# Scan levels of a chunked recurrence: a narrower wait on TensorE, K made in halves by ScalarE, two levels of block copies moved to ScalarE

## What is computed

```python
f = lb + (1.0 - lb) * jax.nn.sigmoid(f_raw);  k = 1.0 - f;  v = i_in
# S_t = diag(f_t) S_{t-1} + k_t v_t^T,   o_t = S_t^T q_t
def step(S, inp):
    qb, kb, vb, gb = inp
    G = jnp.cumsum(gb, axis=-2)
    o_inter = jnp.einsum('bhtd,bhdv->bhtv', qb * jnp.exp(G), S)
    diff = G[:, :, :, None, :] - G[:, :, None, :, :]
    decay = jnp.exp(jnp.where(causal, diff, -jnp.inf))
    A = jnp.sum(qb[:, :, :, None, :] * kb[:, :, None, :, :] * decay, axis=-1)
    o = o_inter + jnp.einsum('bhts,bhsv->bhtv', A, vb)
    ...
```

## Time and profile before

| | |
|---|---|
| median of 3 runs | 2320.0 us (2317.55 to 2323.71) |
| the profiled execution's own time | 2319.5 us |
| its span | 2317.7 us |
| mean granted TensorE clock | 0.976 of full |
| busy: PE / DVE / ACT / POOL | 96% / 37% / 32% / 40% |
| chain that ended last: PE / issue / POOL / DVE / ACT | 60% / 23% / 11% / 4% / 1% |
| the ten levels, first product to the last q update's end | 1709.50 to 1801.76 us |

### The profile page before, as it was taken

How to read it: one execution, slowest core, us unless ns; L and a number is a source line. 1 busy time by engine, 2 the same in 40 slices (tenths; PEclk the granted TensorE clock), 3 DMA queues, 4 the chain that set the end, 5 groups by cost and what they waited for, 6 DMA issues and landing times.

```text
span 2317.7 us, 32862 instructions
## 1 busy us (share of the span) xinstructions
PE 2229.0 (96%) x12905; PEld 1931.1 (83%) x12905; DVE 864.1 (37%) x1286; ACT 750.5 (32%) x1098; POOL 932.4 (40%) x707
## 2 busy tenths in 40 slices
PE   6999999999999999999997999999988999999998
PEld 5888888777888778887876999999988699999887
DVE  4232202666555522222036222232159054555402
ACT  4333212435667433333133322112100323333213
POOL 3444444445220344445433334444335014454542
PEclk9999999999999999999998999999989879999999
DMA  4223222521000223232221222222210002322231
GB/s 154 91 90 97 92 101 91 157 69 59 1 1 2 82 73 96 93 100 91 90 91 55 91 91 90 91 91 90 73 37 1 19 19 84 99 90 90 91 100 64
DMA packets 150638, 178.99 MB, mean 77 GB/s; under 512 B 6949, under 2 KB 140430, under 8 KB 150558
## 3 DMA queue, kind: packets, MB, share of 16 engines
q1 hardware_dynamic: 150395, 177.83, 23.5%
q10 hardware_dynamic: 163, 0.04, 0.0%
HBM read 175.76 MB, written 2.10 MB: 77 GB/s over the span
## 4 chain that ended last, share of the span: by engine, by line
PE 60%; issue 23%; POOL 11%; DVE 4%; ACT 1%; SPq 1%; DMA 0%; POOLq 0%; DVEq 0%; ACTq 0%
PE ps L1628 38%; POOL wlo L621 11%; PE ps L1768 11%; PE ps L2132 2%; PE ps L2155 2%; PE ps L2038 2%; PE ps L2008 1%; PE ps L2024 1%; PE ps L1882 1%; DVE Ad L1542 0%; PE ps L2034 0%; PE ps L2006 0%; PE ps L2089 0%; DVE Tod L1568 0%; PE ps L1861 0%
## 5 line engine op out<-in xcount | busy, mean ns | idle before, releaser
L621 POOL TENSOR_TENSOR wlo<-raw,whi 128x512 fp32r<-128x512 f32 x638 | 838.4, 1347 | 1177.8 <-ACT whi L708 1177.7
L1628 PE MATMUL ps<-xh,whi 128*128 128x512 f32 (+2 forms) x2432 | 702.4, 335 | 23.0 <-DVE gateT L1419 10.2
L1628 PE MATMUL ps<-xh,wlo 128*128 128x512 f32 (+2 forms) x2432 | 699.9, 334 | 0.0
L1628 PE MATMUL ps<-xl,whi 128*128 128x512 f32 (+2 forms) x2432 | 696.9, 333 | 0.0
L708 ACT ACTIVATE whi<-raw 128x2048 fp32r<-128x2048 f32 x160 | 304.9, 1906 | 791.0 <-PE ps L1628 480.8
L1628 PEld LDWEIGHTS ps<-xh,whi 128*128 128x128 f32 x2432 | 414.9, 189 | 75.5 <-POOL wlo L621 8.7
L1628 PEld LDWEIGHTS ps<-xh,wlo 128*128 128x128 f32 x2432 | 413.5, 189 | 46.6 <-issue 1.9
L1628 PEld LDWEIGHTS ps<-xl,whi 128*128 128x128 f32 x2432 | 413.5, 189 | 45.8
L1768 PE MATMUL ps<-act_h,wlo 128*128 (+1 forms) x528 | 208.6, 395 | 0.0
L1768 PE MATMUL ps<-act_l,whi 128*128 (+1 forms) x528 | 208.6, 395 | 0.0
L1768 PE MATMUL ps<-act_h,whi 128*128 (+1 forms) x528 | 208.6, 395 | 0.0
(11 more groups left out here) (301 smaller groups left out, 2582.5 us busy)
## 6 DMA issues: line engine op xcount, KB each, us to landing
raw<-in_w_in SPq DMA_DIRECT2D x47, 1024.0 KB, 5.0
raw<-in_ffn_wg SPq DMA_DIRECT2D x22, 1024.0 KB, 5.2
raw<-in_ffn_wu SPq DMA_DIRECT2D x22, 1024.0 KB, 5.1
raw<-in_ffn_wd SPq DMA_DIRECT2D x22, 1024.0 KB, 4.9
raw<-in_w_up SPq DMA_DIRECT2D x22, 1024.0 KB, 5.1
raw<-in_w_down SPq DMA_DIRECT2D x11, 1024.0 KB, 4.9
raw<-in_w_out SPq DMA_DIRECT2D x8, 1024.0 KB, 5.4
raw<-in_ple_w_gate SPq DMA_DIRECT2D x4, 1024.0 KB, 5.3
```

The lines of the kernel that those rows point to most:

```text
L621: last = nc.gpsimd.tensor_tensor(wlo[:, slot, d], raw[:, slot, d], whi[:, slot, d].bitcast(F32), ALU.subtract)
L1628: last = mm(ps[:, j * banks + b, 0:n], w[:, k, e * P:(e + 1) * P], x[:, k, c0:c0 + n], start=(k == 0 and q == 0), stop=(k == KD - 1 and q ...
```

## The change

Three edits, and the counts of semaphores that follow from them.

1. At levels above 0, PE waits for `LEVEL_UP` of the level below less one: for the q update, not for the decay totals issued behind it. POOL's k update now waits for those totals itself (`lev_up`), which it had got through PE's wait.
2. K = 1 - Fg is made by ACT in two halves of four heads (`k_made`), behind ACT's rounding of a weight unit. PE waits for the half that holds the head (META for both). DVE's instruction is gone, and `lev_up` counts one less.
3. At levels 5 and 6 (runs of 32 and 64 tokens) ACT copies the products into `Ad`, with plain copies of whole blocks, two per head at level 5 and one at level 6. PE waits for their banks on `lev_cp`. DVE has no copy to make at these levels but still waits for the products before its q update.

```diff
--- before.py
+++ after.py
@@ -145,7 +145,7 @@
 
 def level_updates():
 
-    n, out = 1, {}
+    n, out = 0, {}
     for lv in range(-1, LEVELS):
         for g in range(2):
             n += 2 if 0 <= lv < LEVELS - 1 else 1
@@ -165,7 +165,8 @@
 X_BANK = [2, 3, 4, 5, 6, 7, 2, 3]
 LEVEL_SEQ = level_sequence()
 LEVEL_UP = level_updates()
-LEVEL_CP0 = sum(lv < 7 for lv, _, _ in LEVEL_SEQ)
+FIRST_CP = 5
+LEVEL_CP0 = sum(lv < FIRST_CP for lv, _, _ in LEVEL_SEQ)
 P2 = 5
 N_ROWS = sum(len(r) for r in ROWS[1:]) + 2 * len(HEAD_ROWS)
 N_CONST = 7
@@ -426,6 +427,7 @@
         lev_sel = sem("lev_sel")
         lev_up = sem("lev_up")
         lev_k = sem("lev_k")
+        k_made = sem("k_made")
         amx_mm = sem("amx_mm")
         amx_cp = sem("amx_cp")
         o2_mm = sem("o2_mm")
@@ -692,6 +694,8 @@
             for lv in range(LEVELS - 1):
                 for g in range(2):
 
+                    if lv:
+                        pool.wait_ge(lev_up, LEVEL_UP[lv - 1, g])
                     pool.wait_ge(lev_mm, 1 + max(i for i, (l, n, _) in enumerate(LEVEL_SEQ) if l == lv and n in range(HG * g, HG * (g + 1))))
                     k2, decay = k_update(lv, g)
                     nc.gpsimd.tensor_tensor(k2, k2, decay, ALU.mult).then_inc(lev_k, 1)
@@ -1041,7 +1045,19 @@
             for u in range(W_IN2 + 35, W_IN2 + 38):
                 hi_one(u)
 
+            act.wait_ge(tiles_done, used_count(W_IN2 + 35))
+            act.wait_ge(p2_free, P2 + 64)
+            for g in range(2):
+                heads = slice(HG * g, HG * (g + 1))
+                nc.scalar.activation(K[:, heads, :], Fg[:, heads, :], ACT.Copy, scale=-1.0, bias=1.0).then_inc(k_made, 1)
             for idx, (lv, n, bank) in enumerate(LEVEL_SEQ):
+                if FIRST_CP <= lv < 7:
+                    act.wait_ge(lev_mm, idx + 1)
+                    w = 1 << lv
+                    for r in range(0, P, 2 * w):
+                        last = nc.scalar.activation(Ad[r:r + w, n, :].rearrange("p (i t) -> p i t", i=TT)[:, :, r + w:r + 2 * w],
+                                                    ps[r:r + w, bank, :].rearrange("p (i t) -> p i t", i=TT)[:, :, r + w:r + 2 * w], ACT.Copy)
+                    last.then_inc(lev_cp, 1)
                 if lv >= 7:
                     act.wait_ge(lev_mm, idx + 1)
                     w = 256 if lv == 7 else 512
@@ -1521,7 +1537,6 @@
                 ins.then_inc(lev_up, 1)
                 dve.wait_ge(lev_up, up_n[0])
 
-            link(nc.vector.tensor_scalar(K[:], Fg[:], -1.0, 1.0, ALU.mult, ALU.add))
             nc.vector.memset(Am[:], 0.0).then_inc(az, 1)
             dve.wait_ge(az, 2)
             idx = 0
@@ -1536,7 +1551,7 @@
                     if lv < 7 and n == META:
                         nc.vector.copy_predicated(Am[:], levelmask[0:M, lv + 1, 0:M].unsqueeze(1).to_broadcast([M, VH, M]),
                                                   ps[0:M, bank, 0:VH * M].rearrange("p (n m) -> p n m", n=VH)).then_inc(lev_sel, 1)
-                    elif 0 <= lv < 7:
+                    elif 0 <= lv < FIRST_CP:
                         second = lambda x: x.rearrange("p (i b e w) -> p i b e w", i=TT, e=2, w=1 << lv)[:, :, :, 1, :]
                         mask = levelmask[:, lv + 1, :].rearrange("p (b e w) -> p b e w", e=2, w=1 << lv)[:, :, 1, :]
                         nc.vector.copy_predicated(second(Ad[:, n, :]), mask.unsqueeze(1).to_broadcast([P, TT, HD >> lv, 1 << lv]),
@@ -2136,12 +2151,17 @@
             pe.wait_ge(vev, 4)
             last_user = {}
             for idx, (lv, n, bank) in enumerate(LEVEL_SEQ):
-                pe.wait_ge(lev_up, 1 if lv < 0 else LEVEL_UP[lv - 1, META if n == META else n // HG])
+                if lv < 0:
+                    pe.wait_ge(k_made, 2 if n == META else n // HG + 1)
+                elif n == META:
+                    pe.wait_ge(lev_up, LEVEL_UP[lv - 1, META])
+                else:
+                    pe.wait_ge(lev_up, LEVEL_UP[lv - 1, n // HG] - (lv > 0))
                 if lv > 0 and n != META:
                     pe.wait_ge(lev_k, 2 * (lv - 1) + n // HG + 1)
                 if bank in last_user:
                     was, at_lv = last_user[bank]
-                    if at_lv < 7:
+                    if at_lv < FIRST_CP:
                         pe.wait_ge(lev_sel, was + 1)
                     else:
                         pe.wait_ge(lev_cp, was + 1 - LEVEL_CP0)
@@ -2161,7 +2181,7 @@
                         last = mm(ps[:, bank, i * 2 * P:(i + 1) * 2 * P], K[:, n, xc(i)], Q[:, n, xc(2, 2)], start=True, stop=True)
                 last.then_inc(lev_mm, 1)
             pe.wait_ge(lev_up, LEVEL_UP[LEVELS - 1, META])
-            pe.wait_ge(lev_cp, 2 * VH)
+            pe.wait_ge(lev_cp, (LEVELS - FIRST_CP) * VH)
             pe.wait_ge(lev_sel, LEVEL_CP0)
             def meta_scores(n):
```

## The result

The changed kernel takes 2324.66 us (median of 20 runs, 2320.95 to 2330.11), the kernel before 2319.94 us (20 runs, 2315.22 to 2324.36): a ratio of 1.0024, 95% interval 1.0017 to 1.0031, so 4 to 7 us slower. The forecast was 2318, and its range for 8 in 10 went up to 2323.5. The measured time lies above that.

The account below looks back on a forecast made before the run. DVE was taken to lead up to level 3, PE from level 4, with k updates holding DVE. Terms summed to -0.3 us; with the clock and cautious terms, -1.5 us was taken: 2318 us, range 2315 to 2322.5 (8 in 10: 2311.5 to 2323.5).

Parts of the forecast that it names:

- DVE leads up to level 3, PE from level 4, and POOL's k updates hold DVE.: Ten levels: DVE without gaps at first, then PE at 3.65 us a group; SBUF multiplies and k updates run in turn.
- The pattern of held totals: Levels 2 to 4: four decay totals wait behind POOL's k updates, adding 6.8 us; DVE net 2.5 us later.
- Level 6 ends at 1786.4, level 7's second group at 1789.8, level 8 at 1792.9: Times in us for PE; before, they were 1784.28, 1789.36 and 1791.62.
- Edit 2 puts DVE 0.9 us earlier and loses it by level 2: K in halves brings DVE's first copy 0.9 us earlier; a k update moved into level 0's q update uses that up.
- ACT's copies: Levels 5 and 6: about 0.5 us and less than 0.4 us a head, under PE's 0.913 us.
- the third rival: Level 5: ACT's narrow copies cost 0.6 us each, 2.3 us more, giving 2320 us; 5 in 100.
- Level 8 in 6.9 us and the last q update as before: Level 8: eight heads at 0.86 us each take 6.9 us instead of 8.38, ending at 1799.8 instead of 1800.0.
- The last q update and all behind it are as before.: Behind level 8: no change, so the levels' sum of -0.3 us stood for the whole profiled execution.
- It should fall to half speed less often: PE's clock: idle time in more and shorter pieces, so less half clock; part of going from -0.3 to -1.5 us.
- low end of edit 2's gain: K in halves: DVE's first copy comes 0.9 to 1.9 us earlier; the cautious 0.9 was taken.
- The rival on the slower side: Held totals from level 1, DVE behind PE at levels 5 and 6: +5 to +7 us, about 2325.5; 7 in 100.
- The 5 in 100 for slower: Whole kernel: chance of 0.05 given to a measurably slower result, with about 0.3% (7 us) as the threshold.

Follow-up runs that it names:

- write-only kernels: Changed kernel and kernel before, each k update replaced by two POOL memsets of the same part of K: 2311.85 us (ratio 0.9968) and 2310.89 us (0.9962).
- edit 2 alone: Kernel before with only K made in halves by ACT: 2319.68 us, ratio 1.0003.
- kernel before with four memsets: Kernel before with four DVE memsets of 264 columns ahead of the very last q update: 2325.23 us, ratio 1.0023.
- edit 1 alone: Kernel before with PE waiting only for the q update and POOL itself for the totals: 2329.33 us, ratio 1.0049.

## Why the prediction was wrong

- **DVE leads up to level 3, PE from level 4, and POOL's k updates hold DVE.** Right, and the write-only kernels show the reason.
- **The pattern of held totals.** Right in place, and in what it costs: the four totals of the sum were to add 6.8 us, and they took 2.12, 2.00, 1.94 and 1.88 us where free ones take 0.42, 0.29, 0.29 and 0.23, 6.7 us more. It had none held behind level 4, and four were (1.75 to 1.80 us). Level 4's last q update was to end 71.8 us behind the last weight product (1775.4 less 1703.57), and ends at 72.06 us. Before it was 69.5 us.
- **Level 6 ends at 1786.4, level 7's second group at 1789.8, level 8 at 1792.9.** In the same count 82.8, 86.2 and 89.3 us, measured 82.93, 86.33 and 89.23 us. Right.
- **Edit 2 puts DVE 0.9 us earlier and loses it by level 2.** Right: the q update of level 0's second group was held, 3.38 us instead of 1.26. In edit 2 alone it is lost too, there by a total of level 1.
- **ACT's copies.** Right: 0.5 us and less than 0.4 us were estimated, 0.55 and 0.38 us measured, and the third rival falls.
- **Level 8 in 6.9 us and the last q update as before.** Mis-sized. Level 8 took 7.8 us: its two groups of products took 3.72 us each, where the sum had the pace of ACT's copies, 3.4, and between them PE waited 0.35 us for a q update that was held for 2.25 us [the rows at 1793.03 and 1795.34]. The V stage began at 98.94 us, where my sum gives 98.0. The levels cost +0.7 us and not -0.3.
- **"The last q update and all behind it are as before."** This is the step that failed. It put the V stage and the tail at no change without looking at their clock. The V stage is 3.7 us longer and the tail 1.2 us, both by the granted clock alone (half clock for 19.6 us of the stage instead of 12.0). Both come with the start at 98.9 us instead of 98.25, as the kernel before with four memsets shows, which has none of the edits and the same two lengths.
- **"It should fall to half speed less often", for which, together with the low end of edit 2's gain, I took 1.2 us off.** Wrong in sign for the program. It was true in the levels: behind the first products one piece at half clock, in the finer stretches, where there were three. It was not asked of what comes after the levels. That a stage which starts later or earlier by less than 1 us can lose 4 us to the clock was in no term of the sum.
- **The chances.** The rival on the slower side was put on held totals at levels 5 and 6. That is what edit 1 alone shows (+10 us), but in the changed kernel edit 3 prevents it, as I had judged. The loss came from a place that none of the cases held. The 5 in 100 for slower stood for more than 7 us; the loss of 4.7 us lies between that and the top of the range for 8 in 10. A stage in which the clock goes up and down should have widened that range on both sides.

What stays open: why the clock comes and goes in the V stage where it does. The runs show that its length hangs on the start within a few tenths of a us (52.48 us for 98.53, 55.88 us for 98.92), and not by what rule: starts of 96.4 to 98.5 us cost 52 to 54 us, those of 98.9 and 105.5 us 56 us, those of 101.1 and 101.8 us 55 us, and those of 83.9 and 85.6 us (K zero) 58 and 56 us. One thing in the traces' clock records may help whoever looks further: in seven of the kernels a fall to half clock lies 121.4 to 121.5 us behind the last weight product, though their V stages start anywhere from 96.8 to 101.8 us. So that fall did not move with the stage. The V stage's own instructions were not changed in any kernel here. Each V stage's length is from one profile; the medians bear them out only in sum.

## What to carry to other kernels

A wait that looks idle can be what keeps two engines out of each other's way: before taking one away, ask which instruction it lets start earlier, and beside what that will run. Where GpSimd and VectorE both multiply from SBUF, order them so that GpSimd's work stands beside VectorE's PSUM copies; here that won 2.2 us of the levels over the changed kernel. And count a gain to the end of the program: here a later stage in which TensorE is busy but its clock goes up and down turned 0.7 us into 5, and 1.5 us into nothing.

## What the runs showed of the hardware that I had not expected

- The clock's first rise lies 8.8 to 8.9 us behind the last weight product in all fourteen profiles, though products start again at 4.0 us in some and at 5.9 us in others. Here an earlier start bought half-speed work.
- The V stage, PE busy throughout, lasted from 51.8 to 57.8 us with the same instructions. Between starts of 98.53 and 98.92 us its length grows by 3.4 us.
- Of two instructions released by the same products, q and k update, that of POOL began 0.05 us earlier in the two kernels that have edit 3 without edit 1 (q updates of 2.94 to 2.96 us, 1.22 us when free). In the changed kernel that of DVE began 0.01 us earlier (1778.13 beside 1778.14: 1.23 us, then k updates of 3.00 us). In these rows 0.05 us decide whether it is DVE's update that is held, for 1.7 us, or POOL's, for 1.1 us.
